# A two-layer hybrid trunk: the mixer's spatial products and attention scores, moved from one row behind the second gate block to four places inside it

## The reference: what is computed

```python
# branch A: z = causal spatial product over chunks of 128 tokens, 4 groups
z = jnp.einsum('gts,bnsgc->bntgc', w, vc) + b_s.T[None, None, :, :, None]
y_a = u * z.reshape(bsz, s, MIX_W)
# branch B: attention, window 128, 4 query heads of 64, a learned sink per head
sc = jnp.einsum('bnqhgd,bnkhd->bnhgqk', qb, kb) * (HEAD_DIM ** -0.5)
m = jnp.maximum(jnp.max(sc, axis=-1, keepdims=True), sink); p = jnp.exp(sc - m)
# branch D: depthwise convolution of 31 taps, LayerNorm, swish
# the four branches are then gated and merged
gates = jax.nn.sigmoid(h @ w_gate + b_gate).reshape(bsz, s, N_BRANCH, D_MODEL)
merged = jnp.einsum('bsnc,ncd,bsnd->bsd', ys, w_branch, gates)
```

## Time and profile before

| | |
|---|---|
| median of 3 runs | 818.88 us (815.38 to 821.76) |
| the profiled execution, its own time | 823.82 us |
| its span, first to last instruction | 822.1 us |
| PE busy | 795.6 us, 97% |
| DVE busy | 658.4 us, 80% |
| ACT busy | 505.5 us, 61% |
| transfers | 189.88 MB, mean 231 GB/s |
| mean granted TensorE clock | 0.976 |

### The profile page before, as it was taken

The page is one execution under the profiler, slowest core; times in us unless marked ns, Lnnn a source line. Parts: engine busy times, 40 slices in busy tenths (PEclk is TensorE's granted clock), DMA queues, the critical chain, the costliest instruction groups (busy, mean ns, idle before and its releaser), DMA issues. The chain is left out here.

```text
span 822.1 us, 13258 instructions
## 1 busy us (share of the span) xinstructions
PE 795.6 (97%) x4850; PEld 703.2 (86%) x4850; DVE 658.4 (80%) x859; ACT 505.5 (61%) x573; POOL 21.7 (3%) x37
## 2 busy tenths in 40 slices
PE   8999999999999999998999999999999999999996
PEld 8899999998777788787899999999877777777875
DVE  6868996497678999898676899559758998888987
ACT  7535555653666877776644456564547677777763
POOL 4110000000000000000010000000000000000000
PEclk9999999999899999999999999999978999999998
DMA  8776353376218898998754625337422989999894
GB/s 290 260 253 208 135 169 108 103 247 213 104 48 324 315 371 338 340 333 268 252 175 156 238 103 180 103 128 259 152 102 89 347 327 350 337 353 341 316 341 162
DMA packets 80840, 189.88 MB, mean 231 GB/s; under 512 B 12534, under 2 KB 24472, under 8 KB 80792
## 3 DMA queue, kind: packets, MB, share of 16 engines
q1 hardware_dynamic: 80792, 189.23, 65.3%
HBM read 188.15 MB, written 1.05 MB: 230 GB/s over the span
## 5 line engine op out<-in xcount | busy, mean ns | idle before, releaser
L777 DVE TENSOR_TENSOR w_lo<-raw,w_hi 128x2048 fp32r<-128x2048 f32 (+1 forms) x182 | 400.2, 2215 | 74.2 <-ACT w_hi L500 73.6
L500 ACT ACTIVATE w_hi<-raw 128x2048 fp32r<-128x2048 f32 (+1 forms) x182 | 336.9, 1859 | 192.9 <-PE bank L1311 133.6
L1309 PE MATMUL bank<-a_hi,w_hi 128*128 128x256 f32 x688 | 197.2, 287 | 0.6 <-DVE a_lo L842 0.6
L1310 PE MATMUL bank<-a_hi,w_lo 128*128 128x256 f32 x688 | 195.9, 285 | 0.0
L1311 PE MATMUL bank<-a_lo,w_hi 128*128 128x256 f32 x688 | 195.9, 285 | 0.0
L1309 PE MATMUL bank<-w_hi,y_lo 128*128 128x512 f32 x432 | 172.9, 400 | 9.1 <-DVE y_lo L1237 6.0
L1311 PE MATMUL bank<-w_lo,y_lo 128*128 128x512 f32 x432 | 168.8, 391 | 0.0
L1309 PEld LDWEIGHTS bank<-a_hi,w_hi 128*128 128x128 f32 x688 | 133.3, 194 | 1.7 <-issue 1.6
L1310 PEld LDWEIGHTS bank<-a_hi,w_lo 128*128 128x128 f32 x688 | 133.4, 194 | 0.1
L1311 PEld LDWEIGHTS bank<-a_lo,w_hi 128*128 128x128 f32 x688 | 133.3, 194 | 0.0
L1310 PE MATMUL bank<-w_hi,y_hi 128*128 128x512 f32 x288 | 112.5, 391 | 0.0
(11 more groups left out here) (304 smaller groups left out, 900.0 us busy)
## 6 DMA issues: line engine op xcount, KB each, us to landing
raw<-in_w_e_gate SPq DMA_DIRECT2D x72, 512.0 KB, 4.4
raw<-in_w_e_up SPq DMA_DIRECT2D x72, 512.0 KB, 5.9
raw<-in_w_e_down SPq DMA_DIRECT2D x72, 512.0 KB, 5.4
raw<-in_w_gate SPq DMA_DIRECT2D x56, 512.0 KB, 4.5
raw<-in_w_in SPq DMA_DIRECT2D x38, 512.0 KB, 6.5
raw<-in_w_branch SPq DMA_DIRECT2D x16, 512.0 KB, 4.5
raw<-in_w_o SPq DMA_DIRECT2D x16, 512.0 KB, 4.6
raw<-in_w_gate SPq DMA_DIRECT2D x16, 256.0 KB, 2.7
```

What stands on the lines that cost most here:

```text
L500: a.activation(w_hi[:, at.slot(n, PART), 0:w], raw[:, slot, 0:w], ACT.Copy).then_inc(hi_done, 1)
L777: v.tensor_tensor(w_lo[:, part, 0:w], raw[:, slot, 0:w], w_hi[:, part, 0:w].bitcast(F32), ALU.subtract).then_inc(split_done, 1)
L1309: mm(ps, a2[0], b2[0], start=first, stop=False, skip_group_check=shared)
L1310: mm(ps, a2[1], b2[0], start=False, stop=False, skip_group_check=shared)
```

## The change

The row behind gate block 1 is gone. `gate_unit` gets an argument `aside`, a function that it calls after its second and after its fourth k-step. In unit 12 that is `spatial(0)` and `spatial(1)`, each half of the spatial products. In unit 13 it is `scores(0)`, the four scores of the first token block, and `scores(1)`, the eight of the second. The waits go with the work: `qk_t_done`, `sgw_done` and `vn_done` stand ahead of `spatial(0)`, `cols_done` ahead of `scores(0)`. The signal that a unit is used is attached to the unit's last gate matmul, ahead of the part that follows it. No matmul is added or removed, and the programs of DVE, ACT, POOL and SP are the same.

```diff
-                def gate_unit(b, n, k0, tiles):
+                def gate_unit(b, n, k0, tiles, aside=None):
...
                             last = channels((2 * b + f // 2 + 1) % 4, wp, k, kk, f, k == 0, k == KT - 1)
+                        if aside and kk % 2:
+                            aside(kk // 2)
                     last.then_inc(unit_used, 1)
...
-                gate_block(1)
-
-                pe.wait_ge(S("qk_t_done"), T * (l + 1))
...
-                pe.wait_ge(S("sgw_done"), l + 1)
-                pe.wait_ge(S("cols_done"), l + 1)
-                for h in range(NQ):
-                    last = score(bank[4][:, P * h:P * h + P], h, 0, 0)
...
-                last.then_inc(S("sc_tp"), 1)
...
-                pe.wait_ge(S("vn_done"), l + 1)
-                for c in range(CT):
+                def spatial(c):
+                    if c == 0:
+                        pe.wait_ge(S("qk_t_done"), T * (l + 1))
+                        pe.wait_ge(S("sgw_done"), l + 1)
+                        pe.wait_ge(S("vn_done"), l + 1)
                     for t in range(T):
...
-                last.then_inc(S("z_done"), 1)
+                    if c == CT - 1:
+                        last.then_inc(S("z_done"), 1)
+
+                def scores(part):
+                    if part == 0:
+                        pe.wait_ge(S("cols_done"), l + 1)
+                        for h in range(NQ):
+                            last = score(bank[4][:, P * h:P * h + P], h, 0, 0)
+                            if h == 1:
+                                last.then_inc(S("sc_half"), 1)
+                                pe.wait_ge(S("sc_half"), l + 1)
+                        last.then_inc(S("sc_tp"), 1)
+                        return
+                    for i in range(2):
+                        for h in (2 * i, 2 * i + 1):
+                            for tk in range(T):
+                                c = 256 * (h % 2) + P * tk
+                                last = score(bank[5 + i][:, c:c + P], h, 1, tk)
+                        last.then_inc(S("sc_tp"), 1)
+
+                gate_unit(1, G0 + 2, 0, 4, spatial)
+                gate_unit(1, G0 + 3, 4, 4, scores)
                 gate_block(2)
```

More of the change, by code:

```diff
@@ L1466, in score @@
                     return mm(ps, qk_t[r, tq, P * (h % 2):P * (h % 2) + P], qk_t[r, tk, 2 * P:3 * P], start=True, stop=True)
-                pe.wait_ge(S("sgw_done"), l + 1)
-                pe.wait_ge(S("cols_done"), l + 1)
-                for h in range(NQ):
-                    last = score(bank[4][:, P * h:P * h + P], h, 0, 0)
-                    if h == 1:
-                        last.then_inc(S("sc_half"), 1)
-                        pe.wait_ge(S("sc_half"), l + 1)
-                last.then_inc(S("sc_tp"), 1)
[L1476 to L1481, removed]
-                pe.wait_ge(S("vn_done"), l + 1)
-                for c in range(CT):
+                def spatial(c):
[3 more added lines that the diff above has]
+                        pe.wait_ge(S("vn_done"), l + 1)
                     for t in range(T):
```

## The result

The changed kernel took 826.27 us (median of 9 runs, 824.79 to 830.8), the kernel before 821.04 us (median of 9, 815.38 to 823.27). The ratio is 1.0081, 95% interval 1.0054 to 1.0109: slower by 4.4 to 8.9 us, in the middle 6.6. The forecast was 6.2 us more than the kernel before, 825.1 us in all. The profiled execution took 827.8 us and has a span of 826.1 us.

The account below looks back on a forecast made before the run. PE was taken as the bound, with DVE only 1.2 us behind at the sums. Late sums (+3.4 us) and clock falls behind the wait (+2.8) added 6.2 to 818.88, giving 825.1 us, range 819.5 to 829.0.

Parts of the forecast that it names:

- The late scores and the wait: Mixer, each layer: last scores reach DVE 3.45 us later, PE waits 2.6 us for conv_done, sums start 1.7 us late.
- The price of changing the kind of work: Gate block 1 on PE: three more pairs of changes between gate matmuls and small work, 0.54 us a layer.
- The clock at the row comes back: Behind gate block 1: the clock no longer falls at the row, giving back 1.4 us in the first layer, 1.45 in the second.
- The clock behind the wait: At the sums after PE's wait for conv_done: one fall of the clock in each layer, 1.4 us each, +2.8 in all.
- rival B: At the sums: PE waits, clock falls in one layer (823.7 us) or none (822.3); chance 0.37 together.
- The sum: Whole kernel: 3.4 us from late sums plus 2.8 from clock falls, +6.2 us, 825.1 us against the median.
- C: At the sums: no wait for conv_done arises, 2 x 0.9 us are won, 817.1 us; chance 0.07.
- D: Gate block 1 or 2: clock falls all the same, hidden in the wait; 0.05 for its adding something, 825 to 827.
- E: Behind conv_done: late DVE list reaches a second PE wait, such as ahead of the merging, 827 to 830 us; chance 0.08.
- A: At the sums: PE waits and the clock falls behind it in both layers, 825.1 us; chance 0.43.

Follow-up runs that it names:

- experiment 2: Changed kernel, PE's list untouched, with DVE's taps 10 to 13 moved ahead of the mask of the scores: 819.47 us, ratio 0.9975 to the kernel before.
- experiment 9: Kernel before, PE's list untouched, with five extra DVE products into a scratch tile ahead of the mask of the scores: 824.36 us, ratio 1.0073.
- Experiment 6: Changed kernel with scores first in one part, issued in turn from the two row halves, spatial products second: 814.89 us, ratio 0.9965 to the kernel before.
- Experiment 3: Changed kernel with 11 products of ones by ones in each layer ahead of the wait for conv_done: 822.33 us, ratio 1.0050 to the kernel before.
- experiment 4: Kernel before, its one row kept without interleaving but turned round, spatial products ahead of the scores: 822.79 us, ratio 1.0051.
- experiment 10: Kernel before, its one row kept behind gate block 1, with scores in turn from the two row halves: 817.21 us, ratio 0.9982.
- experiment 8: Changed kernel, PE's list untouched, with DVE's taps 10 and 11 moved ahead of the mask of the scores: 821.24 us, ratio 1.0032 to the kernel before.
- experiment 1: Changed kernel with the pairs of parts exchanged, scores in unit 12 and spatial products in unit 13: 819.73 us, ratio 1.0005 to the kernel before.
- experiment 5: Changed kernel with all 12 scores in one part in unit 12, spatial products in two parts in unit 13: 819.29 us, ratio 1.0002 to the kernel before.
- experiment 7: Against the kernel before, all 12 scores between units 12 and 13, spatial products as one row behind unit 13: 820.68 us, ratio 1.0029.

## Why the prediction was right

**The late scores and the wait: right.** DVE idle ahead of L973, forecast about 3 us: 3.54. L978 forecast at 95.35: 95.97. `conv_done` forecast at 132.9: 133.4. PE ready for the sums, forecast at 130.3: 131.0. PE's wait, forecast 2.6 us a layer: 2.54 and 2.57; that this fits so well is partly luck, since both of its ends came 0.5 to 0.7 us later than forecast. Start of the sums, forecast 1.7 us late: 133.54 against 131.19, 2.35 late, and in the second layer 521.82 against 516.41, of which 2.98 had come about ahead of this layer's mixer (its transposes start at 464.14 against 461.16), so 2.4. That it is this chain is shown from both sides: taking the delay off DVE with PE's list unchanged (experiment 2) removes the loss, and putting it on DVE with the old PE list (experiment 9) makes it.

**The price of changing the kind of work: too small.** Three more pairs at 0.18 and the end of the slow group gave a start of block 2 at 94.3; it was 94.89. The step that failed is to count a part as its matmuls plus two edges. The scores took 2.42 us as 12, and 1.40 + 1.64 = 3.04 us as 4 and 8. Experiment 6 shows why: scores of heads 0 and 1 and of heads 2 and 3 use different row halves and run side by side where one kind follows the other, and the split took one such place away. This 0.6 us delayed the last scores and with them `conv_done`. It also took most of the 0.9 us a layer that PE was to gain: of that, 0.2 were left (131.00 against 131.19).

**The clock at the row comes back: right in these two profiles, too much as an average.** There is no half clock from 76 to 133. But the row does not lower the clock each time: of the four rows in this order that were profiled (two in the kernel before, two in experiment 9) three did. In any case the gain is inside the wait, as forecast.

**The clock behind the wait: right, in both layers, and partly luck.** Forecast 1.4 us each; the sums and what follows took 4.32 us against 131.19 to 133.87 = 2.68 before, 1.6 us. Experiment 3 shows that the idle time is needed for it: with products in its place the clock stays. The reason that the prediction gave, the thin products behind the sums, is not what ran in the first layer, where the clock fell ahead of the sums. At this place the waits of 2.5 to 2.7 us were followed by 0.50 four times out of four (the changed kernel twice, experiments 4 and 9 once each), those of 0.7 to 1.6 us none out of five (experiments 4, 9 and 10 once each, 8 twice). But that such a wait always brings the clock down is not so. The prediction's one precedent for "no fall" was the first layer's last expert pass. PE waits there for 2.2 to 2.6 us in all twelve profiles; the half clock follows in seven (experiments 1, 3, 5, 7, 8, 9 and 10) and not in five (both kernels, experiments 2, 4 and 6). Experiment 7, then 6:

```profile
384.28 0.80 PE L1693 MATMUL bank<-a_hi 128*128 128x512 f32 x1 [2.46 <-DVE a_lo L1270]
384.20:387.40 3.20, 3.12 (x7) 0.50 0.61 169
...
385.74 0.50 PE L1693 MATMUL bank<-a_hi 128*128 128x512 f32 x1 [2.59 <-DVE a_lo L1270]
385.70:389.00 3.30, 3.26 (x20) 1.00 0.36 59
```

So the earlier trace rows showed one outcome of two, and rival B, a fall in one layer or none, stays possible for other executions of the changed kernel than the profiled one.

**The sum.** By these measured terms 2 x (2.4 + 1.6) = 8.0 us, forecast 6.2, timed 4.4 to 8.9. Against its own terms the forecast is 1.8 us too small, against the middle of what was timed, 6.6, only 0.4: so close a fit is luck in part. Why the timed difference is under 8.0 is not shown; one possibility is that the clock does not fall behind the wait in every execution. The spans of the two profiled executions differ by only 4.0 us, because the stages outside the mixers vary by themselves. From 200 to 240 us the clock was 0.87 before and 0.91 in the changed kernel, and 3.0 of the first layer's 4.0 us arrive at the second layer; from 595 to 640, in the second layer's routing stage, it was 0.81 against 0.92, 0.11 x 45 = 5.0 us. Profiles with one and the same PE list in the mixer differ as much there: over 590 to 650 the clock was 0.86 in experiment 2 and 0.94 in the changed kernel, 0.86 in the kernel before and 0.94 in experiment 9. These two terms do not add up to the difference exactly; the rest was not followed. That is why the two profiles must be compared at the place of the change and not at their ends.

**Rivals.** C (no wait) fell with the 2.54 us. D (the clock falls in block 1 or 2) did not occur. E (a second wait of PE on a late DVE list) did not either: from 60 to 215 us and from 440 to 590 us the changed kernel's only PE wait on another engine is the one at L1519. A was the case that came in the profiled execution. The run times alone don't settle it: both A's 6.2 us and B's 3.4 + 1.4 = 4.8 for one fall lie between 4.4 and 8.9; B without a fall, 3.4, does not.

## What to carry to other kernels

Work that is spread out to keep an engine fast also changes when its results are ready. Before moving it, look at who reads it, what is queued behind the reader, and how little slack the next signal has: here the row maxima on DVE came 4.1 us late, the slack took up 1.5 us of it, and PE stood still for the other 2.5. Put first what another engine waits for soonest. A repair that worked without touching PE's list is to give the waiting reader later work of its own to do in the gap (experiment 2). And the gain itself was never there to see: with the lateness mended, interleaving alone cannot be told from the kernel before (experiments 1, 2 and 5).

## What the runs showed of the hardware

- Products of 64 rows from different row halves (0 to 63, 64 to 127) run side by side: 12 scores of 128 x 128 in float32 took 2.42 us in the order of heads, of which 0.25 are a stop for a signal, and 1.54 us in turn. Within one half a score takes 0.22 us. In every pair that ran side by side the two results lay in different banks; whether that is needed was not tried.
- TensorE's clock can fall with PE busy all the time: in experiment 7 after 3.1 us of 4-row and 64-column products (0.99, then 0.50), and in another layer of the same execution it stayed at 1.00 behind the same products. What decides between the two stays open. A single profile does not tell whether such a place costs anything on average.
- The same holds for a wait. One of 2.2 to 2.6 us in the last expert pass was followed by the half clock in seven profiles of twelve.
- 22 instructions of useless 128 x 128 products in place of a wait of 2.5 us kept the clock at 1.00 and saved 1.5 us a layer in the profile (experiment 3). The times of the runs agree with it (2.5 us for two layers) and do not show it alone.
